# Query and pooling units of a two-block transformer kernel: a 512- and a 256-column product per weight tile, evacuated by two engines

## What is computed

```
h = modulate(rms_norm(x), shift, scale)              # (256, 2048)
q, k, v, u = split(h @ w_in_2, [1024, 1280, 1536])   # q: 16 heads of 64; u: 1024 pooling channels
q, k = rope_2d(q), rope_2d(k)
attn = softmax(window scores + context scores + sink) @ (v, v_ctx)
pooled = windowed_mean(u, widths 2, 4, 8, 16) - u    # per group of 256 channels
mixed = (pooled @ pool_w) * pool_scale
x = x + gate * (concat(attn, mixed) @ w_out_2)
x = x + gate * (square(relu(h2 @ w_up)) @ w_down)    # h2: the second normed, modulated x
```

## Time and profile before

| | us |
|---|---|
| three runs: lowest, median, highest | 1644.32, 1645.72, 1648.47 |
| profiled execution: its own time | 1645.58 |
| its span in the profile | 1643.9 |
| TensorE busy with products | 1596.9 (97%) |
| VectorE busy | 1198.1 (73%) |
| ScalarE busy | 769.9 (47%) |

### The profile page before, as it was taken

The page is one execution under the profiler, slowest core; times in us unless marked ns, Lnnn a source line. Parts: engine busy times, 40 slices in busy tenths (PEclk is TensorE's granted clock), DMA queues, the critical chain, the costliest instruction groups (busy, mean ns, idle before and its releaser), DMA issues.

```text
span 1643.9 us, 33164 instructions
## 1 busy us (share of the span) xinstructions
PE 1596.9 (97%) x12170; PEld 1487.9 (91%) x12170; DVE 1198.1 (73%) x1756; ACT 769.9 (47%) x1049; POOL 34.0 (2%) x50
## 2 busy tenths in 40 slices
PE   5999999999999999999899999999999999999997
PEld 4899999899999988899799999899989998899986
DVE  7777677788788774788676767776677666556786
ACT  4545444344445554455455454345433553345542
POOL 0000000000001000000000000000000000000000
PEclk9999999999999999999999999999999999999998
DMA  7888888788876677633265656985698655545552
GB/s 289 302 283 289 283 287 286 288 306 332 326 267 218 227 249 301 227 103 116 86 199 190 204 183 212 274 255 186 189 281 250 200 180 191 191 158 187 180 186 108
DMA packets 94552, 372.65 MB, mean 227 GB/s; under 512 B 10016, under 2 KB 10544, under 8 KB 83968
## 3 DMA queue, kind: packets, MB, share of 16 engines
q1 hardware_dynamic: 88656, 333.87, 60.6%
q10 hardware_dynamic: 4608, 33.56, 5.6%
q0 software_dynamic: 1200, 4.02, 0.7%
HBM read 369.30 MB, written 2.10 MB: 226 GB/s over the span
## 4 chain that ended last, share of the span: by engine, by line
issue 72%; PE 22%; DVE 3%; DMA 1%; ACT 1%; POOL 0%; POOLq 0%; SPq 0%; DVEq 0%; ACTq 0%
PE G L437 6%; PE G L439 6%; PE G L438 6%; PE S L737 1%; PE M L750 1%; DVE lo L1262 1%; PE ADA L474 1%; PE S L724 1%; PE ADA L764 0%; PE S L725 0%; DMA resid<-xT_dram 0%; DVE t L1317 0%; PE M L686 0%; DVE resid L1262 0%; DVE t L1502 0%
## 5 line engine op out<-in xcount | busy, mean ns | idle before, releaser
L1262 DVE TENSOR_TENSOR lo<-raw,hi 128x1024 fp32r<-128x1024 f32 x496 | 607.4, 1225 | 204.4 <-ACT hi L895 190.7
L895 ACT ACTIVATE hi<-raw 128x1024 fp32r<-128x1024 f32 x496 | 526.9, 1062 | 481.6 <-PE G L439 273.0
L437 PE MATMUL G<-actA,hi 128*128 128x256 f32 (+1 forms) x2336 | 670.8, 287 | 2.3 <-DVE lo L1262 1.5
L439 PE MATMUL G<-actA,hi 128*128 128x256 f32 x2336 | 659.9, 282 | 0.0
L438 PE MATMUL G<-actA,lo 128*128 128x256 f32 (+1 forms) x2336 | 659.7, 282 | 0.0
L437 PEld LDWEIGHTS G<-actA,hi 128*128 128x128 f32 x2336 | 442.8, 190 | 33.9 <-issue 23.5
L438 PEld LDWEIGHTS G<-actA,lo 128*128 128x128 f32 x2336 | 442.4, 189 | 0.3
L439 PEld LDWEIGHTS G<-actA,hi 128*128 128x128 f32 x2336 | 442.0, 189 | 0.0
L458 PE MATMUL G<-actB,hi 128*128 128x512 f32 x1024 | 355.3, 391 | 0.0
L459 PE MATMUL G<-actB,lo 128*128 128x256 f32 x1024 | 286.7, 280 | 0.0
L458 PEld LDWEIGHTS G<-actB,hi 128*128 128x128 f32 x1024 | 191.5, 187 | 42.1 <-issue 0.3
(11 more groups left out here) (218 smaller groups left out, 1253.4 us busy)
## 6 DMA issues: line engine op xcount, KB each, us to landing
raw<-stream_dram SPq DMA_DIRECT2D x496, 512.0 KB, 4.3
ada_raw<-w_ada_dram SPq DMA_DIRECT2D x64, 1024.0 KB, 7.5
ada_raw<-w_ada_dram ACTq DMA_DIRECT2D x32, 1024.0 KB, 6.4
resid<-xT_dram SPq DMA_DIRECT2D x4, 512.0 KB, 6.9
ctx_tok<-ctx_tok_dram SPq DMA_DIRECT2D x1, 2048.0 KB, 8.3
W<-ctxT_dram POOLq DMA_DIRECT2D x16, 128.0 KB, 3.6
out_dram<-resid SPq DMA_DIRECT2D x4, 512.0 KB, 2.7
ada_raw<-pool_w_dram POOLq DMA_DIRECT2D x1, 1024.0 KB, 5.1
```

The lines of the kernel that those rows point to most:

```text
L437: pe.matmul(wide, hi[:, slot, cols], x[:, k, 0:T + extra], start=(k == 0), stop=False, skip_group_check=True)
L439: m = pe.matmul(bank, hi[:, slot, cols], x[:, k, T + extra:2 * T + extra], start=False, stop=(k == KT - 1), skip_group_check=True)
L895: return act.activation(dst, src, ACT.Copy)
L1262: return dve.tensor_tensor(dst, a, b, op)
```

## The change

The 16 query and pooling units take the 512 + 256 form. `pair_unit` is cut into `pair_half` for each half of the weights, each with a wait of its own for the low part; the MLP's down units go through it too. The result of a unit now lies in both halves of its bank. ScalarE's `half_copy` copies columns 256 to 511 to the destination and counts half_copied; VectorE's `both` waits for that, adds columns 0 to 255 to the destination and counts evac_done. ScalarE's next half_copy waits for evac_done of the unit before.

```diff
-            def pair_unit(at, j, x, ready=None, ready_base=0):
-                pe.wait_ge(lo_done, at.unit(j, 2, 2))
-                pe.wait_ge(evac_done, at.unit(j, -1))
+            def pair_half(at, j, half, x, ready=None, ready_base=0):
+                slot = (2 * j + half) % RING
+                pe.wait_ge(lo_done, at.unit(j, 1 + half, 2))
+                if half == 0:
+                    pe.wait_ge(evac_done, at.unit(j, -1))
                 bank = G[j % 2]
-                for k in range(KT):
-                    slot, n = (2 * j + k // 8) % RING, k % 8
+                for n in range(KT // 2):
+                    k = half * KT // 2 + n
...
-                    pe.matmul(bank[:], hi[:, slot, cols], x[:, k, :], start=(k == 0), stop=False, skip_group_check=True)
+                    pe.matmul(bank[:], hi[:, slot, cols], x[:, k, 0:2 * T], start=(k == 0), stop=False, skip_group_check=True)
                     m = pe.matmul(bank[:, 0:T], lo[:, slot, cols], x[:, k, 0:T], start=False, stop=(k == KT - 1),
                                   skip_group_check=True)
-                    if n == 7:
-                        m.then_inc(w_used, 1)
+                m.then_inc(w_used, 1)
+
+            def pair_unit(at, j, x, ready=None, ready_base=0):
+                pair_half(at, j, 0, x, ready, ready_base)
+                pair_half(at, j, 1, x, ready, ready_base)
...
-                unit(at, 2 * s, actA)
+                pair_unit(at, 2 * s, actA)
...
-                half_unit(at, 2 * s + 1, 0, actA)
+                pair_half(at, 2 * s + 1, 0, actA)
...
-                half_unit(at, 2 * s + 1, 1, actA)
+                pair_half(at, 2 * s + 1, 1, actA)
...
+            def half_copy(at, j, dst):
+
+                act.wait_ge(w_used, at.unit(j, 2, 2))
+                if at.base + j:
+                    act.wait_ge(evac_done, at.unit(j))
+                copy(dst, G[j % 2][:, T:2 * T]).then_inc(half_copied, 1)
+                own(half_copied)
...
-                evacuate(at, 2 * s, y2[:, s % 2])
+                half_copy(at, 2 * s, y2[:, s % 2])
...
-                evacuate(at, 2 * s + 1, upad2[:, s % 2, inner])
+                half_copy(at, 2 * s + 1, upad2[:, s % 2, inner])
...
+            def both(at, j, dst):
+
+                dve.wait_ge(half_copied, turn.next("half"))
+                tt(dst, dst, G[j % 2][:, 0:T], ALU.add).then_inc(evac_done, 1)
+                evacuated(at, j)
...
                 split(at, 2 * s, 0)
+                both(at, 2 * s, y2[:, s % 2])
                 if s:
                     turned_copies()
...
                 tile_scale()
                 split(at, 2 * s + 1)
+                both(at, 2 * s + 1, upad2[:, s % 2, inner])
```

More of the change, by code:

```diff
@@ L225, in program @@
         sq_added = sem("sq_added")
-        x_new = sem("x_new")
+        x_new, half_copied = sem("x_new"), sem("half_copied")
         c_exp, es_ready = sem("c_exp"), sem("es_ready")
```

## The result

| | before | after |
|---|---|---|
| median of 7 runs | 1646.77 us | 1654.76 us |
| profiled execution, own time | 1645.58 us | 1655.67 us |
| its span | 1643.9 us | 1653.9 us |

The ratio of the times is 1.005, with a 95% interval of 1.0037 to 1.0062: about 8.2 us slower, 6.1 to 10.2. One of the seven times of before, 2226.1 us, was disturbed and does not enter the ratio, nor does one of 3997.49 us in a later experiment (the additions in VectorE's idle time); the runs of after lie between 1651.22 and 1656.75 us. The forecast was 1653.8 us.

The account below looks back on a forecast made before the run. TensorE, 97% busy, was taken to bound the kernel before, a loop through VectorE the changed stage. 6.0 + 0.2 + 0.46 + 1.5 = 8.2 us on 1645.58 us gave 1653.8 us, range 1649.5 to 1658.5.

Parts of the forecast that it names:

- The loop: VectorE's chain: 12.67 us from reduction to rotation, 7.59 to the next reduction; 20.26 us a lap, +6.0 over seven laps.
- 7.62 us, half a unit in it: less 0.10: Stretch from rotation to next reduction: the new form shortens the half unit in it by 0.10 us.
- all that the change can give: TensorE's products in the 16 query and pooling units: 0.20 us saved a unit, 3.2 us in total.
- The modulation rows: In two of the seven laps, between rotation and half unit: 1.92 and 1.07 us, 144.8 us instead of 141.8.
- Lap 0 and the end: First lap's rotation, behind the addition: +0.2 us; stage's end, TensorE also waiting for unit 15's addition: +0.46 us.
- The clock: TensorE's clock falls once, behind lap 6's wait before the rotation: 1.5 us; bounds none and two falls (2 x 1.7).
- The waits: TensorE before the rotation, released by VectorE's addition: seven or eight times, 10 to 12 us, longest near 2.6.
- The copies: ScalarE's half copies come early, so VectorE's additions don't wait: 0; upper bound 0.38 + 0.05 us a lap.
- The MLP: Down units wait for the second half's low part in mid-unit: costed at nothing, length unchanged.
- Rival 1: TensorE stays the bound, the rotation's wait hidden, only the 3.2 us gain stands: 1642.4 us; chance 0.07.
- Rival 2: Partly absorbed: additions cost under 0.4 us a lap on VectorE's chain; +3 us, 1648 to 1650; chance 0.15.
- Rival 3: TensorE's clock falls in every lap, 1.5 us behind each of seven waits: 1662.8 us; chance 0.06.

Follow-up runs that it names:

- the first experiment: The changed kernel without VectorE's addition and the high-by-low product, ScalarE evacuating columns 0 to 255: 1643.9 us against 1645.9 for the kernel before, ratio 0.9991.

## Why the prediction was right, point by point

- **The loop.** Right, and the largest term. Forecast were 12.67 us to the rotation and 7.59 from it to the next reduction; they are 12.71 and 7.63, a lap of 20.35 instead of 20.26. The experiments with one more operation on and off the loop, and with the additions elsewhere, show that it is the additions' place on VectorE's queue. A release by VectorE with no addition ahead of it was not run; what a lap would be without the 0.92 us of the two additions, 20.35 - 0.92 = 19.43 us, is an estimate.
- **"7.62 us, half a unit in it: less 0.10"** is the term that was mis-sized, by more than its number says. The 0.10 us came from a stretch with 24 tiles in this stage against 32 tiles in the MLP. Put into this stage, a half unit gains 0.03 to 0.05 us: from an unhindered rotation to the values product are 745.99 - 742.65 = 3.34 us in the kernel without the addition, and 744.52 - 741.15 = 3.37 before (the rows stand with the first experiment). The comparison's 12.6 ns a tile come apart into three: 5 are the gain that the same three half units show in the new form (8.62 - 8.50 us over 24 tiles). 3.3 are the first start: a product behind one of another kind has a longer spacing in both forms, at 748.64 us 0.20 us to the next start instead of 0.12, and the 24 tiles hold one such start and the 32 none. The last 4 are a difference of place: the wide form itself takes (8.50 - 0.08) / 24 = 0.351 us a tile in this stage and 0.347 in the MLP; what makes it so no run shows. The price of "all that the change can give", 3.2 us, was therefore too high: the seven laps of the first experiment give 0.9.
- **The modulation rows**, put in at their durations of 1.92 and 1.07 us, lengthen the first two laps by 3.3 us together over two even laps, 0.3 more than forecast. Together with seven times 0.09 this makes the laps' +6.9 of the +6.0.
- **Lap 0 and the end**: +0.3 and +0.5, forecast +0.2 and +0.46. The wait before lap 0's rotation grew from 0.30 to 0.83 us.
- **The clock**: "I take one, in lap 6, at 1.5 us" did not happen in the profiled execution of the changed kernel, though the wait was 2.41 us for a forecast 2.6. The bounds of none and two held, and the price of 1.54 us was found in another kernel. That the forecast's 8.2 us and the measured 8.2 are equal is luck, they agree better than the terms do: in the profile the clock was 1.5 us too much, the laps, the start and the end 1.1 too little, and the 0.6 won back behind the stage were in no term, which leaves 7.2. Whether a fall happened in some of the timed executions can't be said; only profiled ones have a clock.
- **The waits**, named as signs: eight, as forecast, but 7.7 us in all instead of 10 to 12, with one named as VectorE's and seven as "issue". In lap 7 it is 0.69 us for a forecast 1.3. The 11.7 us there was counted from a reduction (767.51 us) at which VectorE was late, so TensorE was further on than in the other laps. The waits enter no term but the clock's, which rests on lap 6, and there 2.6 was near. A granted clock under 1.00 behind the longest wait did not come.
- **The copies**: no wait from lap 1 on, as taken. **The MLP**: no cost, as taken.
- **Rival 1**, TensorE stays the bound, needed the chain to be shorter by 1.3 us in lap 7 and 2.6 in lap 6. Putting the additions ahead of the subtractions takes 1.26 us off it: lap 7's wait is gone, 1.38 us are left of lap 6's, and the loss can't be told any more. **Rival 2** is refuted by laps of 20.35 us. **Rival 3**: no lap of the changed kernel had a fall; waits of up to 1.45 us had none in the laps of any kernel here.

No version tried here beats the kernel before by more than can be told. The one without the addition leaves out a part of the result, and those with the additions elsewhere come level with it.

## What to carry to other kernels

When an engine is busy to 97%, ask before cutting its work who else would have to do more, and where on that engine's queue the new work would stand: an operation of 0.42 us on VectorE cost a lap nothing where its idle stretch held it, and its full 0.46 us (with the gap to the next) ahead of what TensorE waits for. If a release moves from one engine to another, add up everything that is queued ahead of it on the new one. Take the price of a saving from the stage in which it is to be made: the same tile was worth 0.10 us a half unit by a comparison across stages and 0.04 in its own.

## What the runs showed of the hardware

- A product of 512 columns and one of 256 on one weight tile saved, over three of 256, 0.15 us for 32 tiles in the laps that TensorE bounds, 5 ns a tile. The comparison across stages had 12.6 ns. The Trainium skill ("TensorE: Matmul & The Clock Gate", Back-to-back issue gap), by its fixed 2.5 ns for each product in the isolated case, would have given an estimated 0.08 us for these 32 tiles; the measured value lies between the two.
- Idle stretches of TensorE of the same length, 2.41 us, ahead of the same rotation, were followed by 3 us or so at the clock's lower level (granted clock 0.50, 1.2 GHz) in the kernel with an operation in VectorE's slack and by full clock (1.00) in the changed kernel; one of 1.91 us was followed by a fall, one of 2.31 was not. The Trainium skill ("TensorE: Matmul & The Clock Gate", What's actually happening) says of the slow products at a kernel's start that their number varies from run to run. Whether falls within a kernel vary so from one execution of the same kernel to the next is not shown: each kernel here has one profile.
- The view of waits named "issue" for seven of eight waits whose releaser was VectorE's addition. In lap 6 the rotation followed that addition's end by 0.11 us, and the operation added ahead of it made the laps longer by 0.46 us, its own 0.42 and the gap.
